# Three expert pairs written out behind a loop, a transposed up-projection in a feed-forward, and unused matmuls in a router

## The reference, cut to what matters

```python
h2 = rms_norm(x, norm2_g[l])
f = jnp.square(jax.nn.relu(jnp.einsum('bsd,df->bsf', h2, w_mlp1[l])))   # 1024 -> 4096
x = x + jnp.einsum('bsf,fd->bsd', f, w_mlp2[l])                          # 4096 -> 1024
...
logits = (xt @ w_router).astype(jnp.float32)
top_logit, top_idx = lax.top_k(logits, TOP_K)                            # 2 of 8
gates = jax.nn.softmax(top_logit, axis=-1)
...
def swiglu(h, w_gate, w_up, w_down):                                     # 1024 -> 3584 -> 1024
    return (jax.nn.silu(h @ w_gate) * (h @ w_up)) @ w_down
```

## Time and profile before

| | us |
|---|---|
| median of 3 runs | 1783.53 |
| lowest, highest | 1783.36, 1788.15 |
| the profiled execution, its time | 1787.61 |
| the profiled execution, its span | 1785.8 |
| PE busy | 1720.7 (96%) |
| DVE busy | 1324.7 (74%) |
| ACT busy | 1145.8 (64%) |

### The profile page before, as it was taken

One profiled execution on the slowest core, in us unless ns is written; L12 is line 12 of the kernel. 1 busy time (PEld: TensorE's weight loads), 2 busy tenths in 40 slices (PEclk: granted clock), 3 DMA queues, 4 the chain that ended last, 5 costly groups with the idle time before them and its releaser, 6 DMA issues.

```text
span 1785.8 us, 23061 instructions
## 1 busy us (share of the span) xinstructions
PE 1720.7 (96%) x8476; PEld 1406.6 (79%) x8476; DVE 1324.7 (74%) x1193; ACT 1145.8 (64%) x1198; POOL 71.9 (4%) x78
## 2 busy tenths in 40 slices
PE   7999999989999999979999999999999999999998
PEld 6778888877788886668788878788878788887886
DVE  5764444576554467679888888798898898988987
ACT  5645543665544367667777777677777677776775
POOL 2200000130100010010000000000000000000000
PEclk9999999899999999999999999999999999999999
DMA  9455553644655554249999999999999999999995
GB/s 361 143 176 177 179 180 97 199 146 152 204 178 193 160 172 130 75 151 362 368 343 364 355 321 372 342 349 373 320 352 372 345 365 370 332 365 353 342 370 193
DMA packets 227796, 477.74 MB, mean 268 GB/s; under 512 B 11148, under 2 KB 54512, under 8 KB 227688
## 3 DMA queue, kind: packets, MB, share of 16 engines
q1 hardware_dynamic: 220080, 468.30, 73.9%
q10 hardware_dynamic: 7096, 7.42, 1.4%
q0 software_dynamic: 512, 0.54, 0.1%
HBM read 474.36 MB, written 1.08 MB: 266 GB/s over the span
## 4 chain that ended last, share of the span: by engine, by line
PE 70%; ACT 3%; DVE 3%; issue 3%; DMA 1%; POOL 1%; DVEq 0%; ACTq 0%; POOLq 0%
PE bank L686 21%; PE bank L689 21%; PE bank L687 21%; PE bank L1149 2%; PE bank L1304 1%; PE bank L1262 1%; PE bank L680 1%; ACT w_hi L1874 1%; DMA decay<-decay_dram 1%; POOL decay L642 1%; DVE w_lo L1956 1%; ACT w_hi L1401 0%; PE bank L842 0%; DVE w_lo L2484 0%; PE bank L1276 0%
## 5 line engine op out<-in xcount | busy, mean ns | idle before, releaser
L2484 DVE TENSOR_TENSOR w_lo<-raw,w_hi 128x2048 fp32r<-128x2048 f32 x333 | 757.3, 2290 | 119.5 <-ACT w_hi L1874 110.7
L1874 ACT ACTIVATE w_hi<-raw 128x2048 fp32r<-128x2048 f32 x333 | 633.2, 1919 | 178.0 <-PE bank L689 178.0
L1956 DVE TENSOR_TENSOR w_lo<-raw,w_hi 128x2048 fp32r<-128x2048 f32 (+3 forms) x117 | 253.1, 2168 | 147.1 <-ACT w_hi L1401 146.8
L686 PE MATMUL bank<-w_hi,xg_hi 128*128 128x512 f32 x896 | 354.1, 395 | 6.3 <-DVE w_lo L2484 4.6
L689 PE MATMUL bank<-w_hi,xg_lo 128*128 128x512 f32 x896 | 349.4, 390 | 0.0
L687 PE MATMUL bank<-w_lo,xg_hi 128*128 128x512 f32 x896 | 348.9, 389 | 0.0
L686 PE MATMUL bank<-w_hi,a_hi 128*128 128x512 f32 (+3 forms) x672 | 262.4, 391 | 13.0 <-DVE w_lo L1956 5.2
L1401 ACT ACTIVATE w_hi<-raw 128x2048 fp32r<-128x2048 f32 (+3 forms) x117 | 211.0, 1810 | 88.6 <-PE bank L689 85.6
L687 PE MATMUL bank<-w_lo,a_hi 128*128 128x512 f32 (+3 forms) x672 | 255.3, 380 | 0.0
L689 PE MATMUL bank<-w_hi,a_lo 128*128 128x512 f32 (+3 forms) x672 | 255.0, 379 | 0.0
L686 PEld LDWEIGHTS bank<-w_hi,xg_hi 128*128 128x128 f32 x896 | 168.3, 188 | 41.9 <-DVE w_lo L2484 6.3
(11 more groups left out here) (253 smaller groups left out, 1627.8 us busy)
## 6 DMA issues: line engine op xcount, KB each, us to landing
raw<-in_moe_w_gate SPq DMA_DIRECT2D x112, 1024.0 KB, 7.0
raw<-in_moe_w_up SPq DMA_DIRECT2D x112, 1024.0 KB, 7.1
raw<-in_moe_w_down SPq DMA_DIRECT2D x112, 1024.0 KB, 6.5
raw<-in_w_mlp SPq DMA_DIRECT2D x32, 1024.0 KB, 5.2
raw<-in_ffn_w_gate SPq DMA_DIRECT2D x22, 512.0 KB, 4.0
raw<-in_ffn_w_up SPq DMA_DIRECT2D x22, 512.0 KB, 4.9
raw<-in_ffn_w_down SPq DMA_DIRECT2D x11, 1024.0 KB, 5.0
raw<-in_w_in SPq DMA_DIRECT2D x9, 1024.0 KB, 12.5
```

The lines of the kernel that those rows point to most:

```text
L686: pe.matmul(o, hi, h, start=start, stop=False)
L1874: act.activation(w_hi[:, g % NSPLIT, :], raw_at(g, GRAN), ACT.Copy).then_inc(hi_made, 1)
L1956: dve.tensor_tensor(w_lo[:, g % NSPLIT, 0:n], raw_at(g, n), w_hi[:, g % NSPLIT, 0:n].bitcast(F32), ALU.subtract).then_inc(lo_made, 1)
L2484: dve.tensor_tensor(w_lo[:, g % NSPLIT, :], raw_at(g, GRAN), w_hi[:, g % NSPLIT, :].bitcast(F32), ALU.subtract).then_inc(lo_made, 1)
```

## The change

It has three parts that the title names, and some smaller ones with them.

- **Experts.** `PEELED` = 3: the loop runs one pair, three are written out behind it. `item(pair, v, last)` counts items from the loop's end, with n, u = divmod(v, 2). In the ACT loop a silu of one column stands ahead of the items. `chunk_t(7)` now stands between the two granules down in all items, and in ACT's and DVE's order the split of granule 40 comes ahead of that of the transposed product in all of them. An item's last granule down does one half of the output columns after the other (`down_halves`), and the output is rounded and scattered by halves. `xg_hi` and `xg_lo` are each one tile for both experts, written by one instruction instead of two on ACT and on DVE.
- **First feed-forward.** `upward` has the weights' 128 x 128 tile as the stationary operand and the 256 tokens as the moving one, 48 matmuls a granule, so that the result is transposed already; the transposes of `f_sb` go. The chunks use banks 4 and 5, but chunk 1 banks 6 and 7, and PE waits for `f_made` from chunk 2 on. The scale by `rstd` moves behind the down-projection, squared, as `rstd2` (DVE multiplies by it where it adds the result to the tokens). ACT rounds `f_hi` right behind the squares.
- **Router.** `keep_warm(n)` issues n matmuls 256 wide into bank 3, whose result nobody reads: 15, 7, 16, 13 and 9 of them ahead of five places where PE waits.

```diff
+
+        def up_bank(c):
+
+            return 6 if c == 1 else 4
...
+            def down_halves(g, lhs, kt0):
...
                         cols = slice(kk * D + h * 512, kk * D + (h + 1) * 512)
                         mm = parts3([bank[h][:]], lhs(0, kt0 + kk, 0), lhs(1, kt0 + kk, 0), [w_hi[:, slot, cols]], [w_lo[:, slot, cols]],
                                     False, kk == 1)
-                    mm.then_inc(y_psum, 1)
+                    if h == 0:
+                        mm.then_inc(y_psum, 1)
+                mm.then_inc(w_used, 1)
...
+
+            def upward(g, c, half, middle=None):
+
+                slot = g % NSPLIT
+                for kk in range(4):
+                    if middle is not None:
+                        middle(kk)
+                    hi, lo = (a_at(part, "norm2", 4 * half + kk)[:, 0, :] for part in (a_hi, a_lo))
+                    for k in range(4):
+                        o = bank[up_bank(c) + k // 2][:, k % 2 * S:(k % 2 + 1) * S]
+                        cols = slice(kk * 512 + k * P, kk * 512 + (k + 1) * P)
+                        pe.matmul(o, w_hi[:, slot, cols], hi, start=half == 0 and kk == 0 and k % 2 == 0, stop=False)
+                        pe.matmul(o, w_hi[:, slot, cols], lo, start=False, stop=False)
+                        mm = pe.matmul(o, w_lo[:, slot, cols], hi, start=False, stop=half == 1 and kk == 3 and k % 2 == 1)
+                mm.then_inc(w_used, 1)
+
             for c in range(FF0_CHUNKS + 1):
-                ups = [bank[4 + b][:] for b in range(NB)]
                 if c < FF0_CHUNKS:
-                    if c >= 1:
+                    if c >= 2:
                         pe.wait_ge(f_made, 2 * c)
+                    if c == 1:
+                        norm_ready("norm2", 1)
                     pe.wait_ge(lo_made, g + 1)
-                    across(g, 512, a_tile("norm2"), 0, ups, True, False, at_one(lambda: x_t("norm2", 1)) if c == 0 else None)
+                    upward(g, c, 0, at_one(lambda: x_t("norm2", 1)) if c == 0 else None)
                     g += 1
-                if c >= 1:
+                if c == FF0_CHUNKS:
                     pe.wait_ge(f_made, 2 * c)
-                    for k in range(2):
-                        tstep(t, [f_sb[:, (c - 1) % 2, b, kt * P:(kt + 1) * P] for kt in (2 * k, 2 * k + 1)
-                                  for b in range(NB)])
-                        t += 1
-                if c == FF0_CHUNKS:
                     mem_half(g, 0)
                     g += 1
...
-                    across(g, 512, a_tile("norm2"), 4, ups, False, True)
+                    upward(g, c, 1)
                     g += 1
-                ready = dve_steps(t - 1)
                 t = mem_t(t, c, 1)
                 if c >= 1:
-                    pe.wait_ge(t_dve, ready)
+                    pe.wait_ge(f_lo_made, 2 * c)
...
+            def keep_warm(n):
+
+                for _ in range(n):
+                    pe.matmul(bank[3][:, 0:S], a_at(a_hi, "nffn1", 0)[:, 0, 0:P], a_at(a_hi, "nffn1", 1)[:, 0, :],
+                              start=True, stop=True)
+
             pe.wait_ge(router_lo_made, 1)
             for half in range(2):
                 if half == 1:
                     x_t("nffn1", 1)
+                    keep_warm(15)
                 norm_ready("nffn1", half)
...
             mm.then_inc(r_psum, 1)
+            keep_warm(7)
             pe.wait_ge(r_sb, 1)
...
             mm.then_inc(rt_psum, 1)
+            keep_warm(16)
             pe.wait_ge(ch_made, 1)
...
             mm.then_inc(rk_psum, 1)
+            keep_warm(13)
...
+            keep_warm(9)
+
+            def item(pair, v, last):
+
+                n, u = divmod(v, 2)
...
                     if c == 0:
-                        pe.wait_ge(y_act, pair * 2 + (u + 1))
-                        pe.wait_ge(y_dve, pair * 2 + (u + 1))
-                        scatter()
+                        for half in range(2):
+                            pe.wait_ge(y_act, pair * 4 + (2 * v + half + 1))
+                            pe.wait_ge(y_dve, pair * 4 + (2 * v + half + 1))
+                            scatter(half)
...
                     gathers = u == 1 and c == GATHER_CHUNK and not last
                     if gathers:
-                        pe.wait_ge(pick_made, pair + 2)
+                        pe.wait_ge(pick_made, pair + (n + 2))
                         gather_t(0)
                         gather_t(1)
-                    elif c == GATHER_CHUNK:
-                        chunk_t(c + 1)
                     if c >= 1:
                         t_made(chunk_step(u, c, last) + 1)
                         for half in range(2):
-                            if gathers and half == 1:
-                                gather_t(2)
+                            if c == GATHER_CHUNK and half == 1:
+                                if gathers:
+                                    gather_t(2)
                                 chunk_t(c + 1)
                             pe.wait_ge(lo_made, granules(k + 1))
                             mf_tile = lambda p, kt, b: (mf_hi, mf_lo)[p][:, (c - 1 + u) % 2, kt, :]
-                            if last and u == 1 and c == MOE_CHUNKS and half == 1:
-                                down_last(NG + k, mf_tile, 2)
+                            if c == MOE_CHUNKS and half == 1:
+                                down_halves(NG + k, mf_tile, 2)
                             else:
                                 down(NG + k, mf_tile, 2 * half,
                                      [[bank[0][:], bank[1][:]]], c == 1 and half == 0, c == MOE_CHUNKS and half == 1)
...
-            last_pair = pe.value_load(n_last[0:1, 0:1], min_val=N_EXPERTS // 2 - 1, max_val=N_EXPERTS - 1)
-            with pe.Fori(0, last_pair) as i:
-                for u in range(2):
-                    item(i, u, False)
-            for u in range(2):
-                item(last_pair, u, True)
+            loop_pairs = pe.value_load(n_loop[0:1, 0:1], min_val=N_EXPERTS // 2 - PEELED, max_val=N_EXPERTS - PEELED)
+            with pe.Fori(0, loop_pairs) as i:
+                for v in range(2):
+                    item(i, v, False)
+            for v in range(2 * PEELED):
+                item(loop_pairs, v, v >= 2 * (PEELED - 1))
...
                 if c >= 1:
                     hi_to(first + (2 if c < FF0_CHUNKS else 0))
-                    for k in range(2):
-                        t_hi(t, f_hi[:, (c - 1) % 2, 2 * k:2 * k + 2, :])
-                        t += 1
                 if c < FF0_CHUNKS:
                     hi_to(first + 3)
                     t = mem_hi(t, c, NMEM0)
                     act.wait_ge(w_used, first + 2)
-                    for b in range(NB):
-                        f = f_sb[:, c % 2, b, :]
-                        chained(act.activation(f, bank[4 + b][:], ACT.Relu, scale=rstd[:, NORM2, b:b + 1]))
+                    for q in range(2):
+                        f = f_sb[:, c % 2, q, :]
+                        chained(act.activation(f, bank[up_bank(c) + q][:], ACT.Relu))
                         act.activation(f, f, ACT.Square).then_inc(f_made, 1)
+                    for q in range(2):
+                        act.wait_ge(f_made, 2 * c + q + 1)
+                        act.activation(f_hi[:, c % 2, 2 * q:2 * q + 2, :], f_sb[:, c % 2, q, :].rearrange("p (k s) -> p k s", k=2),
+                                       ACT.Copy).then_inc(f_hi_made, 1)
...
                         if gathers:
                             gather_hi(0)
                             gather_hi(1)
-                            e_hi(k)
-                            k += 1
+                        e_hi(k)
+                        k += 1
+                        if gathers:
                             gather_hi(2)
                         chunk_hi(c + 1)
...
+                ahead = 0 if last and u else AHEAD
+                for k in range(ahead - 1):
                     e_hi(MOE_GRANULES + k)
+                act.wait_ge(y_psum, pair * 2 + (v + 1))
+                y_out(0)
+                act.wait_ge(w_used, pair * (2 * MOE_GRANULES) + (v * MOE_GRANULES + NG + MOE_GRANULES))
+                y_out(1)
+                if ahead:
+                    e_hi(MOE_GRANULES + AHEAD - 1)
...
+            loop_pairs = act.value_load(n_loop[0:1, 0:1], min_val=N_EXPERTS // 2 - PEELED, max_val=N_EXPERTS - PEELED)
+            with act.Fori(0, loop_pairs) as i:
+                act.activation(warm[:, 1:2], eps[:], ACT.Silu)
+                for v in range(2):
+                    item(i, v, False)
+            for v in range(2 * PEELED):
+                item(loop_pairs, v, v >= 2 * (PEELED - 1))
...
                     lo_to(first + (2 if c < FF0_CHUNKS else 0))
-                    for k in range(2):
-                        t_lo(t, f_lo[:, (c - 1) % 2, 2 * k:2 * k + 2, :], f_hi[:, (c - 1) % 2, 2 * k:2 * k + 2, :])
-                        t += 1
```

(5 more changed lines are left out.)

198 lines of the change are left out of this document (90 added, 108 removed).

## The result

The changed kernel took 1756.4 us, the median of four executions (1754.0 to 1760.6), the kernel before 1784.7 (1783.4 to 1788.2): a ratio of 0.9841, 95% interval 0.9817 to 0.9865. That is 28.4 us less. Forecast were a median of 1757.0, and -28.6 for the profiled execution. The profiled execution of after has a span of 1754.5 us, 31.3 under that of before. In five further executions the changed kernel took 1757.2 us, ratio 0.9839 (0.9827 to 0.9852); the experiments are compared with these.

The account below looks back on a forecast made before the run. PE was taken as the bound, busy 1720.7 of 1785.8 us. The terms sum to -28.6 us; from the median 1783.5 that gives 1754.9 with all dips, 1759.8 with none, so 1757 was forecast, range 1749 to 1767.

Parts of the forecast that it names:

- (b): First feed-forward: the transposes go, 0.89 us for eight of them in each of 8 chunks, -7.1 us.
- small +0.1: Stages ahead of transposes: `rstd2` makes four additions on DVE longer, +0.1 us; halved output and `down_halves` 0.
- Transposes of chunk 7: Experts: a granule down fills PE's five waits of about 2.6 us for DVE's product, -13.1 us.
- second rival: Experts: PE waits for `mf_lo` instead of the product, up to 11.3 us, so 1768, likelier 1763; chance 0.10.
- Slow clock behind these stops: Experts: PE's clock dips behind two of the five product waits, 1.6 us each, vanish with the waits, -3.2 us.
- Pair borders: Experts' loop turns: 4.6 us of PE waits for `w_lo` and 0.5 of PE's own turns go, -5.1 us.
- (c): First feed-forward: 768 matmuls of 256 columns replace 384 of 512, 91.8 against 87.0 us, +4.8 us.
- (a): First feed-forward, chunk 1: the 2.84 us wait for `f_made` and 1.70 of slow clock behind it go, -4.5 us.
- Router: Router: unused matmuls keep PE's clock up ahead of the first item, -0.5 us, bounds -1.9 and +1.5.
- Free narrow matmuls: First feed-forward: matmuls of 256 columns cost nothing extra over 512, 0 instead of +4.8, so 1752 us; chance 0.10.
- Borders that keep their 5.1: Experts: written-out code must be fetched too, so pair borders or places between keep 5.1 us, 1762; chance 0.09.
- slower rival: First feed-forward: something other than columns bounds the narrow matmuls, up to +87 us, 1839; decides from pitch 0.161; chance 0.05.

Follow-up runs that it names:

- half-width kernel: The kernel before, with the first feed-forward's 384 up-projection matmuls of 512 columns made 768 of 256: 1791.5 us against 1786.2, ratio 1.0027.

## Why the prediction was right

Every term but the transposes of the first feed-forward (b) and the small +0.1 was tested by a kernel of its own. Part of the agreement in the number is luck: the -28.6 was worked out for the profiled execution, and there it was -31.3. For the medians the forecast was 1757 - 1783.5 = -26.5, with half of the dips guessed in, and it was -28.4.

- **Transposes of chunk 7, -13.1**: confirmed to 0.1 us by putting them back. The cover that I called thin is 0.1 us for the product and 0.5 for `mf_lo`; the second rival did not come, but little separates it.
- **Slow clock behind these stops, -3.2**: right, shown by filling the stops. 1.6 us a dip is what the traces give; the kernel with the transposes put back had three of them in its profile, the one before two, and one of its executions, by its mean clock, about none. What the forecast left out is PE's restart, 0.1 us behind each stop: 16.7 instead of 16.3 us for stops and dips.
- **Pair borders, -5.1**: 6.2 in the two profiles, 5.4 with two turns put back. The reason I leaned on, the exit without a wait, held. This term is 1.1 of the 1.5 us by which the experts gave more than forecast, the restarts are the other 0.4. My 0.23 us for PE's own turn was read at one turn and taken for both: at the other one it is 0.02, and 0 to 0.5 in the kernels with turns put back. What is more than the waits are restarts and short holds of PE in the two chunks behind the turn. What I left open, whether the table loads or the turn cost, is settled for the turn.
- **First feed-forward, -4.5 - 7.1 + 4.8 = -6.8**: -6.7. (c) was measured by itself at 4.6 to 5.2. (a) is 2.0 to 4.2, of which the dip is the uncertain part. (b) I did not measure alone; with (a) at the 4.2 to 4.5 of the profiles the stage leaves 6.8 to 7.1 for it, which is a remainder and not a test.
- **Router, -0.5**: -0.9, within the bounds -1.9 to +1.5; 0.8 to 1.1 by taking the unused matmuls out.
- **Small ones, +0.1**: hidden under the third row of the table, which moves by dips.
- **Rivals.** Free narrow matmuls fall by the half-width kernel. Borders that keep their 5.1 fall. The slower rival did not decide, since 0.1196 is above the floor of 0.112, by 8 ns; that margin was not known beforehand.

What was not right: the prediction counts dips as if a stop had one or not, and only behind stops. The same kernel had them at 370 us in one profile and at 745 in the next, and at 311 us it has one with no stop ahead, behind narrow matmuls. The median of the changed kernel, 1756.4, agrees with the forecast partly because such dips in other stages average out.

## What to carry to other kernels

Where PE waits for a product that another engine makes from PE's own last result, put one unit of work that has to be done anyway in between and check both covers, that of the product and that of what is made behind it. Count a stop of PE at its length plus what the clock takes behind it, and fill it with unused matmuls if nothing useful fits; but find the wait in the trace first, since the same matmuls one granule further on cost their full length. Swapping the operands' roles saves transposes only while the moving side stays wide: with 256 columns the matmuls cost 6% more than with 512, with 128 twice as much.
